# Norms at the borders of a two-layer encoder: who makes the diagonal factors, who makes the weights' low parts, and in which order the pieces go

## The reference, cut to what matters

```
def rmsnorm(x, g):
    y = x * lax.rsqrt(jnp.mean(x * x, axis=-1, keepdims=True) + NORM_EPS)
    return y * g

for l in range(2):
    h = rmsnorm(x, g_pre_mix[l])
    m = mixer(h)                      # input projection, attention, output projection
    x = x + rmsnorm(m, g_post_mix[l])
    h = rmsnorm(x, g_pre_ffn[l])
    x = x + rmsnorm(squared_relu_mlp(h), g_post_ffn[l])
```

## Time and profile before

| what | us |
|---|---|
| median of 3 runs (lowest, highest) | 2983.53 (2983.42, 2986.08) |
| the profiled execution | 2981.82 |
| its span, first to last instruction | 2980.0 |
| TensorE busy | 2828.4 (95%) |
| VectorE busy | 1445.7 (49%) |
| ScalarE busy | 854.2 (29%) |
| GpSimd busy | 664.2 (22%) |

### The profile page before, as it was taken

How to read it: one execution, slowest core, us unless ns; L and a number is a source line. 1 busy time by engine, 2 the same in 40 slices (tenths; PEclk the granted TensorE clock), 3 DMA queues, 4 the chain that set the end, 5 groups by cost and what they waited for, 6 DMA issues and landing times.

```text
span 2980.0 us, 49592 instructions
## 1 busy us (share of the span) xinstructions
PE 2828.4 (95%) x18736; PEld 2703.6 (91%) x18736; DVE 1445.7 (49%) x3550; ACT 854.2 (29%) x1562; POOL 664.2 (22%) x427
## 2 busy tenths in 40 slices
PE   8999999898999999999889999998899999999996
PEld 7888888798999999999878888887899999999996
DVE  6666655557333333333576565555473333333334
ACT  5444433453111111111333333335331111111121
POOL 1111100363212121212320000015431212122123
PEclk9999999998999999999989999999999999999998
DMA  5311111332111110101232111114321101010113
GB/s 187 119 59 56 68 68 67 126 139 95 36 50 35 49 56 28 56 29 56 76 124 77 62 58 58 58 66 143 131 75 50 57 28 56 28 56 35 49 36 120
DMA packets 58574, 210.32 MB, mean 71 GB/s; under 512 B 6953, under 2 KB 16561, under 8 KB 55137
## 3 DMA queue, kind: packets, MB, share of 16 engines
q1 hardware_dynamic: 54928, 173.32, 16.5%
q0 software_dynamic: 3552, 35.73, 3.0%
HBM read 163.36 MB, written 51.97 MB: 72 GB/s over the span
## 4 chain that ended last, share of the span: by engine, by line
PE 85%; DVE 6%; issue 5%; ACT 2%; POOL 1%; DMA 0%; DVEq 0%; ACTq 0%; POOLq 0%; SPq 0%
PE ps L1328 71%; PE ps L1437 4%; PE ps L1455 3%; PE ps L1402 2%; DVE XL L977 2%; PE ps L1451 1%; PE ps L1412 1%; DVE ACC L967 1%; PE ps L1414 1%; PE ps L1315 1%; PE ps L1422 1%; ACT Kh L867 1%; DVE PR L1125 1%; ACT Qh L863 1%; PE ps L1308 1%
## 5 line engine op out<-in xcount | busy, mean ns | idle before, releaser
L1328 PE MATMUL ps<-XH,WH 128*128 128x384 f32 (+1 forms) x3096 | 1029.8, 333 | 17.0 <-DVE WL L1012 11.5
L1328 PE MATMUL ps<-XL,WH 128*128 128x384 f32 (+1 forms) x3096 | 1033.1, 334 | 0.0
L1328 PE MATMUL ps<-XH,WL 128*128 128x384 f32 (+1 forms) x3096 | 1027.1, 332 | 0.0
L548 POOL TENSOR_TENSOR WL<-WS,WH 128x1024 fp32r<-128x1024 f32 x199 | 480.7, 2420 | 1771.1 <-ACT WH L687 1676.4
L1328 PE MATMUL ps<-U,WH 128*128 128x384 f32 (+1 forms) x3072 | 756.6, 330 | 0.0
L1328 PEld LDWEIGHTS ps<-XH,WH 128*128 128x128 f32 x3096 | 588.2, 190 | 25.1 <-issue 21.8
L1328 PEld LDWEIGHTS ps<-XL,WH 128*128 128x128 f32 x3096 | 588.2, 190 | 11.8 <-issue 11.8
L1328 PEld LDWEIGHTS ps<-XH,WL 128*128 128x128 f32 x3096 | 588.0, 190 | 9.4 <-issue 9.4
L1328 PEld LDWEIGHTS ps<-U,WH 128*128 128x128 f32 x3072 | 546.3, 189 | 0.0
L1328 PE MATMUL ps<-U,WL 128*128 128x384 f32 (+1 forms) x1536 | 506.1, 329 | 0.0
L687 ACT CAST WH<-WS 128x1024 fp32r<-128x1024 f32 x209 | 217.9, 1045 | 644.6 <-PE ps L1328 628.2
(11 more groups left out here) (123 smaller groups left out, 2143.5 us busy)
## 6 DMA issues: line engine op xcount, KB each, us to landing
WS<-w_in SPq DMA_DIRECT2D x209, 512.0 KB, 4.4
k_out<-KT SPq DMA_DIRECT2D x16, 672.0 KB, 3.1
x_scr<-XRES POOLq DMA_DIRECT2D x6, 1536.0 KB, 5.4
XRES<-x_scr POOLq DMA_DIRECT2D x6, 1536.0 KB, 7.2
v_out<-VT SPq DMA_DIRECT2D x16, 544.0 KB, 4.8
o_scr<-OT SPq DMA_DIRECT2D x14, 544.0 KB, 2.7
BIAS<-nc_scr SPq DMA_DIRECT2D x8, 672.0 KB, 4.8
toep_scr<-rel_scr SPq DMA_DIRECT2D x1, 5120.0 KB, 22.6
```

Of the source, the lines that this page charges most:

```text
L548: pool.tensor_tensor(WL[u][:, :], WS[STAGE[u]][:, :], WH[u][:, :].bitcast(f32), ALU.subtract)\
L1328: return pe.matmul(bank[:, 0:w], wt, xt, start=m == 0, stop=m == 3 * tiles - 1, skip_group_check=False)
```

## The change

All pieces `post_dg` and `pre_dg` of norms 1 to 4 move from VectorE to ScalarE (three activations with a scale per partition). The low parts of the weights that fall into a border go from GpSimd to VectorE (`low_weights`): four in each OUT, those of t = 12 to 15, and three at the end of the last FF of layer 0. The one table becomes three, `AFTER_OUT` for norms 1 and 3, `AFTER_FF` for 2, `AT_END` for 4, with a time for each chunk; VectorE's part of T0 of layer 1 is written out by hand. GpSimd's power waits in addition until the diagonal of the piece before has been made.

```
-PLAN = {
-    "act": dict(pre_hi0=2.75, pre_sq0=3.25, pre_hi1=3.7, pre_sq1=4.2, pre_rb=8.2),
-    "dve": dict(post_st=0.9, post_dg=1.2, post_x0=1.75, post_x1=2.75, pre_lo=3.75, pre_red0=4.9, pre_red1=5.25,
-                pre_st=6.5, pre_dg=7.6),
-    "pe": dict(post_stat=0.75, post_bc=1.5, pre_stat=6, pre_bc=8),
-    "pool": dict(post_load=0, post_pow=1, post_store=3.6, pre_pow=6.7),
+AFTER_OUT = {
+    "act": dict(post_dg=(-7.3, 1.3, 4.95), pre_hi0=(-5.75, 2.75, 7.4), pre_sq0=(-5.25, 3.25, 7.9), pre_hi1=(-4.8, 3.7, 8.4),
+                pre_sq1=(-4.3, 4.2, 8.9), pre_dg=(-0.4, 7.6, 10.6), pre_rb=(0.6, 8.2, 11.2)),
+    "dve": dict(post_st=(-7.6, 0.9, 4.9), post_x0=(-6.75, 2.0, 6.4), post_x1=(-5.75, 2.75, 7.4), pre_lo0=(-4.75, 3.75, 8.4),
+                pre_lo1=(-4.7, 4.95, 8.5), pre_red0=(-3.6, 5.1, 9.2), pre_red1=(-3.25, 5.25, 9.25), pre_st=(-0.9, 6.5, 10.3)),
+    "pe": dict(post_stat=(-7.75, 0.75, 4.75), post_bc=(-7, 1.75, 5.75), pre_stat=(-1, 6.25, 10), pre_bc=(0.25, 8, 11)),
+    "pool": dict(post_pow=(-7.5, 1, 4.95), post_store=(-4.9, 3.6, 8), pre_pow=(-0.8, 6.7, 10.5)),
 }
-SOONER = {"pre_bc": 1, "pre_rb": 1, "pre_dg": 1, "pre_st": 0.2, "pre_pow": 0.2}
-LAST_TICK = 17
-LATER = [(0, 4, 8), (-8.5, 0, 4)]
+AFTER_FF = {
+    "act": dict(post_dg=(1.9, 6.5, 10.9), pre_hi0=(2.5, 6.9, 12.5), pre_sq0=(2.9, 6.95, 12.9), pre_hi1=(3.5, 7.9, 13.5),
+                pre_sq1=(3.9, 8.5, 13.9), pre_dg=(7.5, 15.9, 16.9), pre_rb=(9.3, 16.5, 16.95)),
+    "dve": dict(post_st=(0.9, 5.1), post_x0=(2.5, 6.9), post_x1=(3.5, 7.9), pre_lo0=(4.5, 8.5), pre_lo1=(4.6, 8.6),
+                pre_red0=(6.2,), pre_red1=(6.25,), pre_st=(7.5,)),
+    "pe": dict(post_stat=(0.75, 6, 10.25), post_bc=(2, 7.25, 11.5), pre_stat=(7.75, 15.6, 16.3), pre_bc=(9.25, 16.6, 16.9)),
+    "pool": dict(post_load=(0, 4, 8), post_pow=(0.95, 4.9, 8.9), post_store=(3.95, 8.5, 14), pre_pow=(6.9, 15.5, 16.5)),
+}
+AT_END = {
+    "act": dict(post_dg=(1.2, 5.2, 9.2)),
+    "dve": dict(post_st=(0.9, 4.9, 8.9), post_x0=(1.75, 5.75, 9.75), post_x1=(2.75, 6.75, 10.75)),
+    "pe": dict(post_stat=(0.75, 4.75, 8.75), post_bc=(1.75, 5.75, 9.75)),
+    "pool": dict(post_load=(0, 4, 8), post_pow=(1, 5, 9), post_store=(3.6, 7.6, 11.6)),
+}
+LAST_TICK = 13
 def norm_pieces(engine, n, start, end):
-    at = [(t + LATER[n % 2][c] - (SOONER.get(what, 0) if c == 2 else 0), c, what) for what, t in PLAN[engine].items() for c in range(3)
-          if what.split("_")[0] in NORMS[n]]
+    plan = AT_END if n == 4 else AFTER_OUT if n % 2 else AFTER_FF
+    at = [(t, c, what) for what, ticks in plan[engine].items() for c, t in enumerate(ticks)]
...
# GpSimd, the powers
                     pool.wait_ge(sem["st"], j + 1)
+                    wait(pool, "dg", j)
# GpSimd, OUT and FF
-                        if t % 8 >= 4:
-                            lo_unit(sec, None, 4 * (t // 8) + t % 4, t % 4)
+                        if 4 <= t < 8:
+                            lo_unit(sec, None, t - 4, t - 4)
-                            if t >= 8 and t - 8 < sec.nxt:
+                            if t >= 8 and not sec.last:
                                 lo_unit(sec, i, 4 + t - 8, t - 8)
# ScalarE
+                if what.endswith("dg"):
+                    j = JOBS.index((n, c, what[:-3]))
+                    act.wait_ge(sem["pw"], j + 1)
+                    act.wait_ge(sem["rb"], j - 1)
+                    for q in range(-(-w // P)):
+                        v = min(P, w - q * P)
+                        ins = act.activation(DG[0:v, j % 2, q * P:q * P + v], ident[0:v, 0:v], ACT.Copy, scale=RS[0:v, q:q + 1])
+                    ins.then_inc(sem["dg"], 1)
+                    return
# ScalarE, FF down: hi_unit of step t now stands ahead of the step's two squares
# VectorE, T0 of layer 1
-                    for s in range(9):
-                        dve.wait_ge(sem["D"], sec.at(None, "D", s + 1))
-                        scaled(2, s // 3)
-                        empty_qkv(s, ps[:, s % 6, :])
-                        if s >= 7:
-                            low_weights(sec.loaded + s - 7, s - 7)
-                        norm_at(2, NORM_ON + s)
+                    def empty_next(*steps):
+                        for s in steps:
+                            dve.wait_ge(sem["D"], sec.at(None, "D", s + 1))
+                            scaled(2, s // 3)
+                            empty_qkv(s, ps[:, s % 6, :])
+                    def pieces(c, what):
+                        for step in what.split():
+                            norm(2, c, step)
+                    pieces(2, "post_st")
+                    empty_next(0, 1)
+                    pieces(2, "post_x0")
+                    empty_next(2)
+                    pieces(2, "post_x1 pre_lo0 pre_lo1")
+                    pieces(1, "pre_red0 pre_red1 pre_st")
+                    pieces(2, "pre_red0 pre_red1 pre_st")
+                    empty_next(3, 4, 5, 6, 7)
+                    low_weights(sec.loaded, 0)
+                    empty_next(8)
+                    low_weights(sec.loaded + 1, 1)
# VectorE, OUT and last FF
                         norm_at(1 + 2 * sec.layer, t - OUT_TICK)
+                        if t >= 12:
+                            low_weights(sec.loaded + t - 8, t - 12)
...
+                            if sec.last and 9 <= t and t - 9 < sec.nxt:
+                                low_weights(sec.loaded + 4 + t - 9, t - 9)
# TensorE, end of T0
+                    if sec.layer == 1:
+                        norm_until(2, NORM_ON + 8, 0.25)
```

More of the change, by code:

```diff
@@ L913, in _ @@
                             c, u = t // 4, t % 4
+                            if t >= 8 and u < sec.nxt:
+                                uses = {0: 3, 3: 4}.get(u, 2)
+                                hi_unit(sec, i, 4 + u, u, uses, sec.at(i, "D", 12 + 2 * (t + 1)))
                             for v in (2 * t, 2 * t + 1) if sec.last else ():
@@ L916, in _ @@
                                 square(2 + 2 * sec.layer, v, ct(ACC, c, v % 8)).then_inc(sem["sqo"], 1)
-                            if t >= 8 and u < sec.nxt:
-                                uses = {0: 3, 3: 4}.get(u, 2)
-                                hi_unit(sec, i, 4 + u, u, uses, sec.at(i, "D", 12 + 2 * (t + 1)))
                             if sec.last:
```

## The result

| kernel | median us (lowest, highest) | ratio to before, 95% |
|---|---|---|
| before | 2983.42 (2980.91, 2986.08) | |
| changed | 2953.48 (2951.25, 2955.43) | 0.9902 [0.989, 0.9914] |

A forecast was written before the change was run, and what follows sets the result against it. TensorE, busy 95% of the span, bounds the kernel; only its waits can be won. Gains 11.7 x 2 + 13.2 - 0.4 = 36.2 us off the profiled 2981.8 give 2945.6, as a median 2947, range 2936 to 2970.

The forecast's parts named there:

- Output borders: The two borders from output projection to MLP, layers 0 and 1: a gain of 11.7 us each.
- Then at full clock: Output borders, after the 1.0 wait at chunk 0's pre-norm sum: 12.3 us of work to chunk 1's post-norm factor at 693.7.
- a lower clock there falls into the waits: Output borders, remaining 7 to 8 us of short waits: a lower clock adds nothing, since VectorE's chain sets the pace.
- the clock at 1.00 from 674 to 694: Sign expected in the profile after: TensorE's granted clock stays full over the start of the first output border.
- Part 2: Weights' low parts to VectorE: 1.22 us each against GpSimd's 2.6, ending the stretching of VectorE's XL operations.
- I leave 1.5 of the 5.8: VectorE's XL of chunk 1 lost 5.8 us beside GpSimd; its remaining sums would still cost 1.5, so 4.3 are won.
- XL near 0.55 each: Sign expected in the profile after: VectorE's XL operations take about 0.55 us each.
- Middle: Border between the layers, first sum to first attention score: 16.0 us won in waits less 2.8 for clock, gain 13.2.
- ScalarE's queue: Rival: factors waiting for power hold up ScalarE's copies and casts, 9.4 us each; chance 0.03 about none, 0.03 slower.
- The second sum there waits 1.97 ... whatever TensorE does before: At the end: the second sum waits for GpSimd behind VectorE, so that wait of 1.97 us stays regardless of TensorE's order.
- the first rival: Short waits keep the clock low (8 us more) and VectorE stays stretched (4.3 three times): 2968 us, chance 0.14.
- Part 1: Diagonal factors to ScalarE, 1.0 us each there against VectorE's 0.64 alone or 2.79 beside GpSimd; VectorE spared 1.3 per output border.

The follow-up runs named there:

- e3: The changed kernel with factors back on VectorE and low parts back on GpSimd, so only the new orders against the kernel before: 2967.86 us, 0.9948.
- e6: The changed kernel plus matmuls whose results nobody reads, issued ahead of eleven border pieces to keep TensorE busy in its waits: 2945.84 us, 0.9873.
- e10: The changed kernel with the end as before, unread matmuls in eight waits, and ScalarE's middle factor of chunk 1 ahead of two squares: 2944.07 us, 0.9875.
- e11: The changed kernel run again unaltered: 2951.25 us, 0.9895; its profiled execution took 2956.36.
- e5: The changed kernel with the end as before: its factors on VectorE, TensorE's factor pieces 18 products after their sums instead of 24: 2949.7 us, 0.9888.
- e9: The changed kernel with all factors back on VectorE, that of chunk 1 in the middle right ahead of the first low part: 2958.65 us, 0.9921.
- e1: The changed kernel with all 21 diagonal factors back on VectorE at ScalarE's ticks, orders and low parts as changed: 2957.75 us, 0.9918.
- e4: The kernel before with only the 21 factors moved to ScalarE, at the old ticks: 2981.66 us, 0.9993.

## Why the prediction came out as it did

Sign and mechanism were right: TensorE's waits at the borders were the price, and the orders, the largest part of the gain (e3), move its pieces to where their inputs are ready. The median, 2953.5, is 6.5 above the forecast and inside its range. In the profiled execution 36.2 were forecast and 30.6 came (2981.8 to 2951.25). By the terms of the sum:

**Output borders, 23.4 forecast, 18.8 measured.** The milestones held. I had 1.0 of wait left at the pre-norm sum of chunk 0: 1.59. The post factor of chunk 1 was to start 40.6 after the border's first sum: 41.2 at border 3, 42.8 at border 1. The sum of chunk 2 was to come at 84.9: 85.40 and 87.01. The leftover short waits (7 to 8) are 5.1 and 6.4. With the clock kept (e6) a border wins 11.9, which is the forecast's 11.7. **The step that failed is the clock at these borders, which I put at nothing:** "Then at full clock" behind the first wait, and "a lower clock there falls into the waits" for the rest. Behind the wait of 1.59 the half clock hits products ahead of VectorE's part, so VectorE starts late too; this happened at border 1 and not at border 3, against the sign "the clock at 1.00 from 674 to 694". Behind that of 1.98 at the border's last sum it falls into the MLP, where TensorE never waits. Both are paid in full: 1.7, and 1.6 and 1.5, which is the shortfall (e6). Inside VectorE's part the sentence held: behind the wait of 2.74 the clock was at 0.55 (711.8 to 715.6), at border 3 behind the same wait it was not, and the two borders' last factors and sums lie as far apart after it as before it.

**Part 2 inside it.** "I leave 1.5 of the 5.8": nothing had to be left on XL of chunk 1, which runs at 2.19 for four. GpSimd's sums now meet VectorE's updates and low parts, and mostly it is GpSimd that waits. Timeline of GpSimd in the changed kernel:

```profile
697.11 0.88 POOL L599 TENSOR_TENSOR RB<-RB,SQ 128x320 f32<-128x320 f32 x1 [2.48 <-ACT SQ L739]
703.82 2.06 POOL L599 TENSOR_TENSOR RB<-RB,SQ 128x320 f32<-128x320 f32 x1 [5.83 <-ACT SQ L739]
```

The sum that starts at 703.82 ends 0.7 after VectorE's update (703.39 + 1.76), as if it had begun there: 2.06 instead of 0.88; VectorE loses 0.7, on the low part behind (1.91 for 1.21). With the rule of the Trainium skill ("SBUF — State Buffer", section Who interferes with whom) that the port pair these two engines share is an exclusive lock, the trace agrees: the sum went on when the update ended. Its cost to VectorE stayed under the 3.3 that I had worked out by it, since VectorE came first. "XL near 0.55 each" was right for chunks 1 and 2 and wrong for chunk 0, whose eight still take 11.73, with GpSimd's low parts of the first half beside them.

**Middle, 13.2 forecast, 15.5 measured.** The gap at the tail was to be 7.0 in parts: 0.4 + 0.5 + 2.71 + 3.06 = 6.7. The wait for XL of chunk 2 was to be 1.8: 1.82. Not foreseen: 2.56 at the post factor of chunk 1. The rows of ScalarE, and of GpSimd and VectorE beside it:

```profile
1482.91 0.47 ACT L739 ACTIVATE SQ<-ACC 128x320 f32<-128x320 f32 x1 [1.85 <-POOL RB L599]
1483.29 0.97 ACT L717 ACTIVATE DG<-ident,RS 128x128 f32<-128x128 f32 x3
```

```profile
1478.35 0.88 POOL L576 TENSOR_TENSOR RS<-ST,halfpow 128x3 f32<-128x3 f32 x1 [1.38 <-DVE ST L970]
...
1480.64 4.85 POOL L599 TENSOR_TENSOR RB<-RB,SQ 128x320 f32<-128x320 f32 x3
```

The power was there at 1479.2, the factor was made at 1483.3: ahead of it in ScalarE's queue stood a square that waited for GpSimd's sums, which VectorE's reductions (1480.11, 2.00 for 1536 columns) stretched to 4.85 for three (and themselves, from 3.3 to 4.5: 2.00 + 1.50 + 1.03 for 1.75 + 0.96 + 0.56 at the first border). This is the rival "ScalarE's queue", at one factor of 21 and for 2.6, not 9.4. In e10, with the factor ahead of two squares, 0.61 at a PSX and 0.85 at the next factor are left, and the middle is 0.6 shorter: most of the 2.56 came back as these and other waits. Against it stands what I had deducted and what didn't come in this execution: 2.8 for the clock, which was at 1.00 there (in e11 1.5 of them came), and waits of 4.1 in four places, of which 1.45 came. That the middle came out within 2.3 is in part luck: one term missing, two too large.

**End, 0.4 of loss forecast, 2.3 measured.** "The second sum there waits 1.97 ... whatever TensorE does before" was wrong: it waits 3.01, since TensorE waits less at the factor before. The "full clock" behind the wait of 1.97, by which I argued against the first rival, was so in that trace, but can't be counted on: in e5 it was at 0.61 behind the same wait. The lower clock is at least 1.3 (e6). The other 0.9 aren't cleanly split: in e6 the factors come 0.4, 0.8 and 1.5 later after the first sum than in e5, so not by 0.35 on the last alone, but 1.0 of the 1.5 are e6's own matmuls, which ended after the factor was ready.

**The rest** is 0.8 of span in the untouched stretches and 0.7 around the span. **Part 1** I had priced by VectorE's time, 1.3 at an output border. That was there, 1.0 to 1.5 (e9, e1), but the clock behind the last wait took it back. It pays in the middle, 6.5, where I had no price for it: 1.9 by the factor's place in VectorE's queue and 4.6 since that queue is full (e9). Without the new order it pays nothing in sum (e4).

The first rival (clock low and VectorE stretched, 2968) was half right: of its 8 us of clock 3.5 beyond my 2.8 came (6.3 in all, by e6), of its stretched XL of chunk 1 nothing.

**Open:** why the same wait of 1.6 is followed by full clock once and by half clock another time. The matmuls and the waits around are the same, and no run here tells what differs.

## What to carry to other kernels

When a wait on the bounding engine is shortened, price the clock after it apart from the wait, and ask whether what runs at the lower clock stands ahead of the engine that sets the pace: then it is paid in full. Where the wait can't go, work that nobody reads can keep the clock (6.3 us here), if it ends before the wait does: where it ended after, it held up a factor by 1.0. Move an operation off an engine whose queue is full even where it takes longer elsewhere (1.0 for 0.64), and look at what stands ahead of it in the new queue, and at what that waits for. Before dividing a gain among parts by traces, see whether each profiled execution is near its kernel's median. And an operation whose own price is higher elsewhere (1.2 on VectorE for one low part) can be cheap there if it stretched others (6.3) where it was.

## What the runs showed of the hardware

Waits of TensorE as short as 1.4 us (1.40 at border 3 in e9, 1.57 in e5) were followed by a granted clock at its lower level in some executions or at one border, and not in others of the same kernel; each such time cost 1.5 to 1.7 us, unless, as at the end in e5 and behind the 2.74 at border 1, a wait behind it took it in. Added matmuls in the wait (four in 1.05 us, then 0.70 idle) left it at 1.00; at the end of e6, with 22 of them and then 2.11 idle, it fell all the same. A load of 1.3 MB beside a store of 1.5 MB gained little from a start 1.0 sooner: it took 8.3 us instead of 7.6.
